# Stick-breaking attention in six batches of 512 columns in the accumulator banks, and layer 0's mixer output by token block

## What is computed

```python
z = einsum('bhqd,bhkd->bhqk', q, k) * scale
mask = key_pos < q_pos
log_stay = where(mask, log_sigmoid(-z), 0.0)
suffix = cumsum(log_stay, axis=3, reverse=True) - log_stay
a = where(mask, exp(log_sigmoid(z) + suffix), 0.0)
out_sb = einsum('bhqk,bhkd->bhqd', a, v)
...
mix = concatenate([out_sb, out_gla * silu(g_g)], axis=-1)   # GLA normalised per head first
x = x + mix @ w_out
```

## Time and profile before

| what | us |
|---|---|
| median of 3 runs (1682.12 to 1685.51) | 1683.68 |
| the profiled execution | 1686.56 |
| its span | 1684.8 |
| TensorE busy | 1453.7 (86%) |
| VectorE busy | 980.7 (58%) |
| ScalarE busy | 678.5 (40%) |
| GpSimd busy | 655.1 (39%) |
| gathers, DMA share | 77.4% of 16 engines' span |

### The profile page before, as it was taken

One profiled execution on the slowest core, in us unless ns is written; L12 is line 12 of the kernel. 1 busy time (PEld: TensorE's weight loads), 2 busy tenths in 40 slices (PEclk: granted clock), 3 DMA queues, 4 the chain that ended last, 5 costly groups with the idle time before them and its releaser, 6 DMA issues.

```text
span 1684.8 us, 14521 instructions
## 1 busy us (share of the span) xinstructions
PE 1453.7 (86%) x4326; PEld 712.9 (42%) x4326; DVE 980.7 (58%) x2484; ACT 678.5 (40%) x1854; POOL 655.1 (39%) x537
## 2 busy tenths in 40 slices
PE   6999699997777898989978897989988888897776
PEld 5665466652222333433334444444434343342222
DVE  1132656775777756644446755564654676776744
ACT  1572334443444534333234442532333453444433
POOL 2000234544665343434424342332433543445673
PEclk9999899998999999999989998999999998999999
DMA  5323799999999999999999999999999999999996
GB/s 204 110 100 112 286 357 422 417 410 422 421 421 421 370 423 423 423 422 423 423 421 421 369 420 382 425 413 357 423 423 422 419 421 424 421 421 421 421 422 280
DMA packets 82190, 637.54 MB, mean 378 GB/s; under 512 B 9264, under 2 KB 9408, under 8 KB 10560
## 3 DMA queue, kind: packets, MB, share of 16 engines
q0 software_dynamic: 73728, 536.90, 77.4%
q1 hardware_dynamic: 8064, 98.65, 14.2%
q10 hardware_dynamic: 320, 1.07, 0.2%
HBM read 635.53 MB, written 1.05 MB: 378 GB/s over the span
## 4 chain that ended last, share of the span: by engine, by line
PE 48%; DMA 30%; DVE 9%; ACT 5%; issue 4%; POOL 3%; DVEq 0%; ACTq 0%; POOLq 0%
DMA ring<-in_peer_uv,experts 28%; PE acc L1338 27%; PE work L1139 7%; PE work L1124 6%; DVE ring L1018 5%; POOL ring L533 3%; PE work L1114 3%; PE acc L1303 1%; DMA weights<-in_c_w_in 1%; PE work L1153 1%; ACT diag L704 1%; PE work L1322 1%; ACT gelus L702 1%; DMA weights<-in_peer_w_q 1%; DMA x<-in_x 1%
## 5 line engine op out<-in xcount | busy, mean ns | idle before, releaser
L1338 PE MATMUL acc<-ring,diag 128*128 128x512 f32 x2048 | 992.4, 621 | 179.2 <-ACT diag L704 177.9
L533 POOL DMA_INDIRECT ring<-in_peer_uv,experts x512 | 644.7, 1259 | 887.9 <-PE acc L1338 743.6
L1018 DVE CUSTOM_DVE_ANT_0 ring<-ring,h 128x1024 f32<-128x1024 f32 x512 | 623.0, 1225 | 410.8 <-DMA ring<-in_peer_uv,experts 402.0
L1338 PEld LDWEIGHTS acc<-ring,diag 128*128 128x128 f32 x2048 | 377.3, 196 | 715.8 <-ACT diag L704 368.9
L701 ACT ACTIVATE gelus<-dots 128x1 f32<-128x1 f32 x512 | 102.7, 201 | 636.1 <-DVE dots L1018 635.5
L704 ACT ACTIVATE diag<-ident,gelus 128x128 f32<-128x128 f32 x512 | 205.6, 402 | 16.7
L1124 PE MATMUL work<-weights,hT 128*128 128x512 f32 x352 | 169.3, 614 | 10.2 <-DMA weights<-in_c_w_in 10.2
L702 ACT ACTIVATE gelus<-gelus,gates 128x1 f32<-128x1 f32 x512 | 150.8, 294 | 16.6
L1139 PEld LDWEIGHTS work<-hT,weights 128*128 128x128 f32 x896 | 110.6, 195 | 31.0 <-issue 25.2
L1139 PE MATMUL work<-hT,weights 128*128 128x128 f32 x896 | 111.0, 278 | 5.0 <-DMA weights<-in_peer_w_q 5.0
L1124 PEld LDWEIGHTS work<-weights,hT 128*128 128x128 f32 x352 | 69.1, 198 | 96.4 <-issue 84.5
(11 more groups left out here) (173 smaller groups left out, 765.4 us busy)
## 6 DMA issues: line engine op xcount, KB each, us to landing
weights<-in_c_w_in SPq DMA_DIRECT2D x16, 2048.0 KB, 11.7
weights<-in_peer_w_q SPq DMA_DIRECT2D x11, 2048.0 KB, 12.2
weights<-in_c_w_out SPq DMA_DIRECT2D x8, 2048.0 KB, 11.8
weights<-in_ab_w_in SPq DMA_DIRECT2D x6, 2048.0 KB, 8.0
ring<-in_peer_uv,experts POOLq DMA_INDIRECT x512, 14.5
weights<-in_ab_w_out SPq DMA_DIRECT2D x2, 2048.0 KB, 7.7
keysT<-in_peer_keys SPq DMA_DIRECT2D x2, 1024.0 KB, 10.1
z<-in_peer_w_q SPq DMA_DIRECT2D x1, 2048.0 KB, 7.7
```

The source lines that it names most:

```text
L533: pool.indirect_dma_start(ring[:, step % SLOTS, :], None, uv_rows, bass.IndirectOffsetOnAxis(ap=experts[:, b, step:step + 1], axis=0))\
L1018: nc.vector.tensor_tensor_reduce(out=ring[:, k, 0:D], in0=ring[:, k, 0:D], in1=h[:, b, :], scale=1.0, scalar=0.0, op0=ALU.mult, op1=ALU.ad ...
L1338: last = nc.tensor.matmul(acc[2 * b + n][:, :], diag[:, k, :], ring[:, k, D + n * CH:D + (n + 1) * CH], start=False, stop=True, skip_group ...
```

## The change

`MIX0` is split into stages of their own, so that `PLAN` gives their order. The 24 tiles of 128 keys by 128 queries (8 for block 0, 16 for block 1) are done in six batches of four tiles: batches 0 and 1 are block 0's, each of the others two heads of block 1. A batch's scores go into an `acc` bank and stay there (`STICKZ`); the suffix sums are added onto them in place (`STICKE`), the mask is added in PSUM, and the exponential reads PSUM. Batches 4 and 5 use the banks of 2 and 3. Outputs (`SOUT`), GLA reads and output projection are ordered by token block, block 0 first. `GLAOUT` 1 stands behind `OADD` 0 and `NORM`. Tensors in the ring lie in other slots, so that those read last lie in the upper half; GpSimd waits for `out_full` 3 ahead of the fifth gather. Two of four `before` and `beyond` masks are dropped. The core of the diff:

```diff
-N_MASKS = 16
+N_MASKS = 14
...
+def in_batch(i):
+    if i < 2:
+        return [(hd, 0, 0) for hd in range(4 * i, 4 * i + 4)]
+    return [(hd, kb, 1) for hd in (2 * i - 4, 2 * i - 3) for kb in range(NBLK)]
+STICK_BANK = (0, 1, 2, 3, 2, 3)
...
-        + [("PROJQK",), ("SPATIAL",), ("STICK0",), ("PROJV",), ("QKEYS", 0), ("MIX0",),
-           ("OUT", 0, 0, 0), ("GLAREAD",), ("OUT", 0, 1, 0), ("GLAOUT", 0), ("OUT", 0, 0, 1), ("GLAOUT", 1), ("OUT", 0, 1, 1),
-           ("OADD", 0), ("NORM", "ffn0", (0,)),
+        + [("PROJQK",), ("SPATIAL",), ("STICKZ", 0), ("STICKZ", 1), ("PROJV",), ("RANK",), ("QKEYS", 0), ("STICKZ", 2),
+           ("STICKE", 0), ("ALPHA",), ("STICKZ", 3), ("STICKE", 1), ("GQ",), ("STICKE", 2), ("STICKZ", 4), ("GK",),
+           ("STICKE", 3), ("STICKZ", 5), ("GG", 0), ("STICKE", 4), ("KD",), ("GG", 1), ("STICKE", 5), ("GS",),
+           ("GV", 0), ("GV", 1), ("WOUT",), ("SOUT", 0), ("KV",),
+           ("OUT", 0, 0, 0), ("GLAREAD", 0), ("OUT", 0, 1, 0), ("GLAOUT", 0), ("SOUT", 1), ("GLAREAD", 1),
+           ("OUT", 0, 0, 1), ("OUT", 0, 1, 1), ("OADD", 0), ("NORM", "ffn0", (0,)), ("GLAOUT", 1),
            ("OUT", 1, 0, 0), ("TRANSPOSE", (0,), "ffn0"), ("HTAKE", (0,), "ffn0")]
...
+                        if t == SLOTS // 2:
+                            pool.wait_ge(out_full, 3)
...
+            def stick_soft(i):
+                act.wait_ge(scores_full, i + 1)
+                w, s = acc[STICK_BANK[i]], stick[:, i % 3, :]
+                link(nc.scalar.activation(s, w[:, :], ACT.Abs))
                 link(nc.scalar.activation(s, s, ACT.Exp, scale=-1.0))
                 nc.scalar.activation(s, s, ACT.Ln, bias=1.0).then_inc(soft_ready, 1)
+            def stick_prob(i):
+                act.wait_ge(exp_ready, i + 1)
...
+                nc.scalar.activation(dst, w[:, :], ACT.Exp).then_inc(prob_ready, 1)
...
+            def stick_log(i):
+                dve.wait_ge(soft_ready, i + 1)
...
+                last = nc.vector.scalar_tensor_tensor(s, w[:, :], 0.0, s, ALU.max, ALU.add)
+                link(last)
+                nc.vector.tensor_tensor(own, own, before.unsqueeze(1).to_broadcast(shape), ALU.mult).then_inc(log_ready, 1)
+            def stick_mask(i):
+                dve.wait_ge(sums_full, i + 1)
...
+                nc.vector.tensor_tensor(own, own, beyond.unsqueeze(1).to_broadcast(shape), ALU.add).then_inc(exp_ready, 1)
...
+            def gla_out(n, b):
+                pe.wait_ge(gla_states, 1 if b == 0 else 3)
+                pe.wait_ge(scores_masked, 2 * (b + 1))
...
+            def stick_score(i):
+                if i >= 4:
+                    pe.wait_ge(prob_ready, i - 1)
+                w = acc[STICK_BANK[i]]
+                for k, (hd, kb, qb) in enumerate(in_batch(i)):
+                    last = nc.tensor.matmul(w[:, k * P:(k + 1) * P], kz[:, hd, kb * P:(kb + 1) * P],
+                                            qT[:, hd // 2, qb * P:(qb + 1) * P],
+                                            start=(k == 0), stop=True, skip_group_check=True)
+                last.then_inc(scores_full, 1)
+            def stick_sums(i):
+                pe.wait_ge(masks, N_MASKS)
+                pe.wait_ge(log_ready, i + 1)
+                w, s = acc[STICK_BANK[i]], stick[:, i % 3, :]
+                last = nc.tensor.matmul(w[:, :], suffix[:, 0, :], s, start=False, stop=True, skip_group_check=True)
+                if i >= 2:
+                    for j in range(2):
+                        last = nc.tensor.matmul(w[:, 2 * j * P:(2 * j + 1) * P], suffix[:, 1, :],
+                                                s[:, (2 * j + 1) * P:(2 * j + 2) * P], start=False, stop=True,
+                                                skip_group_check=True)
+                last.then_inc(sums_full, 1)
+            def stick_out(n, b):
+                pe.wait_ge(prob_ready, BATCHES if b else 2)
...
```

More of the change, by code:

```diff
@@ L28 @@
 WB = 4
[L33 to L51, removed]
+BATCHES = 6
 N_CONSTS = 2
-N_MASKS = 16
+N_MASKS = 14
 IDENT_MASKS = 2
@@ L599, in gla_piece @@
[L599 to L627, removed]
@@ L658, in _ @@
                     last.then_inc(free[(bank + 3) % WB], 1)
-                elif kind == "STICK0":
-                    stick_soft(bank, 0)
+                elif kind == "STICKZ":
+                    stick_soft(args[0])
+                elif kind == "STICKE":
+                    stick_prob(args[0])
                 elif kind == "PROJV":
@@ new lines, in stick_out @@
+            def stick_out(n, b):
+                pe.wait_ge(prob_ready, BATCHES if b else 2)
+                w = claim_bank(pe, n)
+                for j in range(4):
+                    for r in range(2):
+                        hd = 2 * j + r
+                        rows, cols = slice(64 * r, 64 * r + 64), slice(hd * SBD, (hd + 1) * SBD)
+                        for kb in range(b + 1):
+                            prob = prob1[:, hd, kb, :] if b else prob0[:, hd, :]
+                            last = nc.tensor.matmul(w[rows, j * P:(j + 1) * P], v_sb[:, kb, cols], prob,
+                                                    start=(kb == 0), stop=(kb == b))
+                last.then_inc(full[n % WB], 1)
@@ L1282, in _ @@
                         tall(bank + b, chunk, hT, b)
-                elif kind == "MIX0":
-                    mix0(bank, chunk, at.banks["PROJV",])
+                elif kind == "STICKZ":
+                    if args[0] == 0:
+                        own_copies(at.banks["PROJQK",], 4)
+                    stick_score(args[0])
+                elif kind == "STICKE":
+                    stick_sums(args[0])
+                elif kind == "RANK":
+                    gate_input(bank)
+                elif kind == "ALPHA":
+                    own_copies(at.banks["RANK",], 1)
+                    gate_logits(bank)
+                elif kind == "GQ":
+                    wide(bank, await_chunk(pe, chunk), slice(0, T), range(0, 2))
+                elif kind == "GK":
+                    wide(bank, await_chunk(pe, at.chunk - 1), slice(0, T), range(2, 4))
+                elif kind in ("GG", "GV"):
+                    tall(bank, chunk - args[0], hT, args[0])
+                elif kind == "KD":
+                    gla_keys(bank)
+                elif kind == "GS":
+                    gla_scores(bank)
+                elif kind == "KV":
+                    own_copies(at.banks["KD",], 2)
+                    gla_sums(bank, [BANKS["GV", b] for b in range(NBLK)])
+                elif kind == "SOUT":
+                    if args[0] == 0:
+                        own_copies(at.banks["PROJV",], NBLK)
+                    stick_out(bank, args[0])
                 elif kind == "GLAREAD":
-                    gla_out(bank)
-                elif kind == "STICK0":
-                    own_copies(at.banks["PROJQK",], 4)
-                    stick_score(bank, 0)
+                    own_copies(BANKS["GV", args[0]], 1)
+                    gla_out(bank, args[0])
                 elif kind == "GLAOUT":
                     b = args[0]
-                    own_copies(at.banks["GLAREAD",] + b, 1)
+                    own_copies(at.banks["GLAREAD", b], 1)
                     fill_transposed(bank, og[:, b, :])
```

324 lines of the change are left out of this document (140 added, 184 removed).

## The result

The changed kernel takes 1697.64 us (median of 4 runs, 1694.14 to 1698.89) against 1683.16 for the kernel before on the same chip, a ratio of 1.0076 with a 95% interval of 1.0059 to 1.0094: slower by 14.5 us, 10 to 16 by the interval. The forecast was 1696.0 and slower.

What follows compares the result with a forecast made beforehand. From about 210 us a stream of gathered expert rows bounds the kernel, so the first gather's shift carries to the end: +6.9 - 2.2 + 7.6 = +12.3 us on 1683.68 gives 1696.0, range 1687 to 1700.

Steps and rivals of the forecast that it cites:

- rival C: Gather stage: a later start closes the stream's early loss of 6.4 us, leaving +5.9 us, 1689.6; 6 in 100.
- Term 1: TensorE's stick-breaking scores and sums: fewer columns, 12.0 us instead of 17.3, so -5.2 us.
- Term 2: TensorE before L1252: the old 1.11 us stall, its half speed and a few small gaps go, -3.2 us.
- Term 3: TensorE ahead of batch 4's scores: waits for ScalarE's probabilities of batch 2 to free the bank, +9.2 us.
- Term 4: TensorE ahead of batch 5's scores: waits for probabilities 3 to free the bank, +3.65 us, bounds 3 and 4.5.
- Term 5: TensorE at half speed after each of the two bank waits, 2 x 1.9 = +3.8 us, bounds 0 and 4.2.
- Front: Stretch up to the end of GV 1: terms add to +8.3 us, following the queues gives +6.9, which was taken.
- Term 6: End of the mixer, from GV 1 to the add after block 0's last OUT: -2.2 us.
- Term 7: Third wait, late GLAOUT 1 behind OADD 0 and NORM: +5.65 us and +1.9 of half speed, bounds 4.5 and 8.5.
- rival A: ScalarE keeps up, probabilities 2 ready when TensorE arrives: +3.6 us, 1687.3; 13 in 100.
- Rival B: TensorE from STICKZ 4 to GLAOUT 1: no new wait seen, only columns count, -10.6 us, 1673.1; 7 in 100.
- Rival D: ScalarE drains at each switch of table: seven more gaps ahead of probabilities 2, +9.0 us, 1705; 2 in 100.

Runs made afterwards that it cites:

- e8_old_filler: Kernel before with two matmuls of 512 columns added ahead of head 0's scores, to fill TensorE's wait there; 1684.44 us, ratio 0.9993 to before.
- e7_queue: Changed kernel with STICKE 2 ahead of GQ, so three gate exponentials stand behind batch 2's probabilities on ScalarE; 1695.90 us, ratio 1.0066 to before.
- e1_tail: Changed kernel with GLAOUT 1 back ahead of OUT(0,1,1), as before the change; 1690.61 us, ratio 1.0031 to before.
- e3_both: Changed kernel with batches 4 and 5 in the banks of 0 and 1, and GLAOUT 1 ahead of OUT(0,1,1); 1673.63 us, ratio 0.9928 to before.
- e2_banks: Changed kernel with batches 4 and 5 in the banks of batches 0 and 1 instead of 2 and 3; 1682.19 us, ratio 0.9984 to before.
- e6_order: Changed kernel, its own banks kept, with STICKZ 4 behind GK and STICKZ 5 behind GG 0; 1681.97 us, ratio 0.9985 to before.
- e4_filler: Changed kernel with eight unread matmuls of 512 columns ahead of the wait for batch 2's probabilities; 1696.31 us, ratio 1.0064 to before.

## Why the prediction was right

The mechanism, the three places and the sign held. By its steps:

- **Bound.** A shift of the first gather is a shift of the end: the table above. The early loss of the stream stayed, the ninth gather 26.55 us behind the first; rival C falls. The rate was read too early: the sixth slice has 357 GB/s, and 420 comes with the seventh, from 253 us. Nothing in the sum hangs on it.
- **Term 1**, -5.2: scores and sums take 12.7 us from start to start at full clock where 12.0 were counted, some tenths of handover at each batch that column counts leave out.
- **Term 2**, -3.2: too small. The old stall is gone with the half speed behind it (1.7 us by e8_old_filler), and so is the half speed of the values' projection, which the prediction kept: 13.90 us instead of 15.4. This 1.5 us is the largest single error of the front.
- **Term 3**, +9.2: the wait was 7.84. TensorE came at 81.1 instead of 82.7, ScalarE's stretch from the scores of batch 2 to probabilities 2 took 69.05 to 88.89 = 19.8 us instead of 20.7. What stands in that stretch was read off the stage list correctly, and e7_queue shows that it sets the end.
- **Term 4**, +3.65: 3.63.
- **Term 5**, +3.8: 0.88 and 0.66 behind the first wait, 0.87 and 1.92 behind the second, 4.3.
- **Front**, +6.9: GV 1 ends 5.0 us later, or 6.0 from scores 0. The projection makes it 1.5 us less than forecast and ScalarE's stretch 0.9 less; half speed makes it 0.5 more and the handovers of term 1 about 1.0. The prediction's own terms add to +8.3, its walk along the queues to +6.9, and the reason given for the difference points the wrong way: a gain of term 2 that does not come would make the front dearer, not cheaper. The walk was the sounder of the two.
- **Term 6**, -2.2: from the end of GV 1 to VectorE's last add for OADD 0, 167.09 - 139.94 = 27.15 us against 28.34, -1.2. The columns were right; the two SOUT, the transposes and the reads take 0.1 to 0.2 us more each than their columns.
- **Term 7**, +7.6: wait 5.59 (5.65 forecast), block 0's transposes start 11.84 us after that add starts, 3.9 before: +8.0. On the old kernel alone it cost 7.3, and undone in e1_tail it gave back 7.5.
- **Sum**, +12.3 on the first gather: 11.7, or 12.7 from scores 0. In the median it is 14.5, and 12.3 lies in its interval of 10 to 16. That the sum is as close as 0.4 us is in part luck: from scores 0 the front came out 0.9 too dear, terms 6 and 7 1.0 and 0.4 too cheap.
- **Chances.** The 0.85 for slower holds only 0.05 of rival A's 0.13 (0.72 + 0.06 + 0.02 + 0.05), less than the "most" that the text names.

Rival A, that ScalarE keeps up, falls with the 7.84 us. Rival B, faster, had its condition made true in e3_both: with none of the three new waits it stands 11.3 us under the before of that chip, where B said 10.6. Rival D, a drain at each switch of table, would have shown as gaps behind the loads; the row at 79.42 starts 0.02 us after the load that began at 78.12 ended. The Trainium skill, Perfetto Trace Analysis, section Matmuls, says that independent groups should rotate through different banks. The runs agree and give it a size: used again two batches later the banks cost the front 16.3 us against four batches later (end of GV 1 from scores 0, changed kernel against e2_banks), where no wait for them is seen. By e6_order 6.9 us of other matmuls between sums and next use does nearly the same, 1.2 us short of it.

Not settled: why the changed kernel's median stands 14.5 us above while its first gather is 11.7 later. The kernel before itself had medians of 1683.16, 1684.93, 1685.5 and 1685.65 beside the four groups of runs, so 2 to 3 us are within the spread, and no run here tells noise from cause at that size.

## What to carry to other kernels

Where all engines walk one list of stages, a new wait for a buffer costs what the other engine has in its queue ahead of the release, not what the releasing instruction takes: write down both queues up to that point before choosing which buffer to use again, and put independent matmuls between. A step that looks off the path (GLAOUT 1, four transposes) cost 7.3 to 7.5 us once its inputs stood behind another chain in the same queues and it stood ahead of the work that used to fill that time. Less work on two engines did not pay here while it made them wait for each other; the same batches, with two banks chosen otherwise and one stage put back, are worth 11 us.

## What the hardware showed that was not expected

The granted clock did not follow the length of an idle time in any simple way. After 1.90 us idle ahead of head 0's scores the kernel before is at half speed (granted clock 0.52 from 50 to 53 us; 1.7 us lost with the scores); after 1.79 us at the same place the changed kernels never are, in seven profiles. The old stall of 1.11 us is followed by half speed in the kernel before (0.68 from 76 to 80 us, some 1.7 us lost), and the same stall of 1.12 us by none in e8_old_filler (1.00 over the same times), where the only thing added is two matmuls some 27 us earlier. In e7_queue 1.98 us idle are followed by a GQ block of 8.36 us instead of 7.07 (1.7 us lost with the sums ahead of it), and 2.40 us idle ahead of batch 4 by a GK block of 7.07, full speed. Behind one and the same wait of 5.59 us OUT(1,0,0) took between 4.7 and 5.5 us in six profiles, 1.3 to 2.1 more than at full speed. Behind the one of 3.63 us batch 5's scores and the gate block lost 1.4, 1.7, 2.8 and 3.0 us in four profiles, behind the one of 7.84 us batch 4's scores and GK 1.5 and 2.1 in two.

So the price of half speed after an idle time of 1.1 to 2.4 us was 0 or about 1.7, and after a longer one 1.3 to 3.0; what decides between them is not shown. Keeping TensorE busy through the wait (e4_filler, 0.97 us left; e8_old_filler, 0.19 left) gave full speed both times it was tried.
